# The first block's mixer: half of the conditioning's steps on GpSimd, a new order on VectorE, and the gate's rows ahead of the state's products

## The reference

```python
# first stage, two blocks (l = 0, 1); the second block's feed-forward is a mixture of 8 experts
mod = c @ w_ada[l] + b_ada[l]        # the "conditioning": 6144 columns, six parts of 1024
h = x * (1 + scale) + shift
p = h @ w_in[l]                      # retention q,k,v,gate | state's x,B,C,z,dt | attention q,k,v
mixed = [retention(...), ssd(...), window_attention(...)] @ w_out[l]
x = layernorm(ALPHA * x + (1 + gate) * mixed)
x = layernorm(ALPHA * x + (1 + gate2) * ffn(modulated x))
# second stage: two more blocks (mLSTM, convolution, cross-attention, feed-forward)
```

## Time and profile before

| | |
|---|---|
| median of 3 runs | 2784.83 us |
| the profiled execution | 2773.45 us |
| its span, first to last instruction | 2771.6 us |
| TensorE busy | 2663.4 us (96%) |
| VectorE busy | 2196.3 us (79%) |
| ScalarE busy | 1520.4 us (55%) |
| GpSimd busy | 50.1 us (2%), 83 instructions |
| TensorE's mean granted clock | 0.972 of full speed |

### The profile page before, as it was taken

How to read it: one execution, slowest core, us unless ns; L and a number is a source line. 1 busy time by engine, 2 the same in 40 slices (tenths; PEclk the granted TensorE clock), 3 DMA queues, 4 the chain that set the end, 5 groups by cost and what they waited for, 6 DMA issues and landing times.

```text
span 2771.6 us, 37886 instructions
## 1 busy us (share of the span) xinstructions
PE 2663.4 (96%) x15712; PEld 2363.7 (85%) x15712; DVE 2196.3 (79%) x2513; ACT 1520.4 (55%) x1567; POOL 50.1 (2%) x83
## 2 busy tenths in 40 slices
PE   6889999979999999999999989999999999999998
PEld 5778998768888888888888779999899999998898
DVE  7877777768888898988888878895487789954777
ACT  3424345437767777677777755544455564444554
POOL 2000000000000000000000000000000000000000
PEclk9879999999999999999999999999999999999999
DMA  8739875269999999999999943446355543544453
GB/s 311 250 129 339 321 250 175 96 198 363 349 356 349 349 360 347 360 347 357 349 360 345 365 157 106 134 152 210 127 199 183 174 149 115 168 152 154 166 183 114
DMA packets 376065, 669.86 MB, mean 242 GB/s; under 512 B 26825, under 2 KB 199503, under 8 KB 371023
## 3 DMA queue, kind: packets, MB, share of 16 engines
q1 hardware_dynamic: 358400, 662.55, 68.0%
q10 hardware_dynamic: 17487, 4.83, 0.7%
HBM read 663.13 MB, written 4.19 MB: 241 GB/s over the span
## 4 chain that ended last, share of the span: by engine, by line
PE 85%; DVE 9%; ACT 2%; issue 1%; DMA 1%; POOL 0%; ACTq 0%; DVEq 0%; POOLq 0%
PE PS L444 24%; PE PS L446 24%; PE PS L445 24%; PE PS L544 2%; DVE LO L439 2%; PE PS L1629 2%; PE PS L2464 2%; DVE AR L2753 1%; DMA RAW<-in_w_ada_dram 1%; PE PS L1860 1%; ACT HI L430 1%; PE PS L2350 1%; PE PS L1896 1%; DVE RAW L697 1%; DVE AR L697 1%
## 5 line engine op out<-in xcount | busy, mean ns | idle before, releaser
L439 DVE TENSOR_TENSOR LO<-RAW,HI 128x2048 fp32r<-128x2048 f32 x410 | 930.7, 2275 | 238.0 <-ACT HI L430 237.9
L430 ACT ACTIVATE HI<-RAW 128x2048 fp32r<-128x2048 f32 x410 | 780.2, 1904 | 351.2 <-PE PS L446 307.2
L444 PE MATMUL PS<-X1H,HI 128*128 128x256 f32 (+1 forms) x2128 | 610.7, 287 | 10.6 <-DVE X1L L584 4.8
L445 PE MATMUL PS<-X1L,HI 128*128 128x256 f32 (+1 forms) x2128 | 604.5, 284 | 0.0
L446 PE MATMUL PS<-X1H,LO 128*128 128x256 f32 (+1 forms) x2128 | 604.4, 284 | 0.0
L444 PE MATMUL PS<-HI,X1H 128*128 128x512 f32 x1056 | 431.1, 408 | 3.5 <-DVE LO L439 3.5
L444 PEld LDWEIGHTS PS<-X1H,HI 128*128 128x128 f32 (+1 forms) x2128 | 408.8, 192 | 15.8 <-issue 8.6
L446 PE MATMUL PS<-HI,X1L 128*128 128x512 f32 x1056 | 414.0, 392 | 0.0
L445 PE MATMUL PS<-LO,X1H 128*128 128x512 f32 x1056 | 413.0, 391 | 0.0
L445 PEld LDWEIGHTS PS<-X1L,HI 128*128 128x128 f32 (+1 forms) x2128 | 408.9, 192 | 2.0
L446 PEld LDWEIGHTS PS<-X1H,LO 128*128 128x128 f32 (+1 forms) x2128 | 408.7, 192 | 0.7
(11 more groups left out here) (392 smaller groups left out, 2891.9 us busy)
## 6 DMA issues: line engine op xcount, KB each, us to landing
RAW<-in_w_in_dram SPq DMA_DIRECT2D x66, 1024.0 KB, 5.2
RAW<-in_expert_w_gate_dram SPq DMA_DIRECT2D x66, 1024.0 KB, 5.2
RAW<-in_expert_w_up_dram SPq DMA_DIRECT2D x64, 1024.0 KB, 5.2
RAW<-in_expert_w_down_dram SPq DMA_DIRECT2D x62, 1024.0 KB, 5.4
RAW<-in_ffn_w_up_dram SPq DMA_DIRECT2D x55, 1024.0 KB, 5.6
AR<-in_expert_w_down_dram SPq DMA_DIRECT2D x50, 1024.0 KB, 5.4
AR<-in_expert_w_up_dram SPq DMA_DIRECT2D x48, 1024.0 KB, 5.5
AR<-in_expert_w_gate_dram SPq DMA_DIRECT2D x46, 1024.0 KB, 5.3
```

Of the source, the lines that this page charges most:

```text
L430: a.activation(HI[:, n % NH, 0:size(i)], raw_at(i), ACT.Copy).then_inc(*hi.up(i))
L439: v.tensor_tensor(LO[:, m % NH, 0:n], raw_at(i), HI[:, m % NH, 0:n].bitcast(F32), ALU.subtract).then_inc(*lo.up(i))
L444: t.matmul(o, lh, rh, start=first, stop=False)
L445: t.matmul(o, lh, rl, start=False, stop=False)
```

## The change

1. **Half of the steps on GpSimd.** The odd steps (columns 1024 to 2047) go to GpSimd. `scalar_tensor_tensor` is replaced there by two instructions: a multiply in place in the landing slot, and an addition. VectorE keeps the even steps. GpSimd does k = 0 to 8 from the mixer's start, k = 9 and 10 between the root for `retvar` and that for `ssdvar`, k = 11 to 15 behind that one, ahead of the residual's roots.
2. **VectorE's order.** The splits, the rotation, the softmax's maxima and the decays of `dve_mixer1` stand in another order, for both blocks. Before, `ada()` did a pair; now one step, spread over sixteen places, four of them behind `dve_fm_scaled`; the last one stands behind the split of the feed-forward's first gate tile and ahead of the residual.
3. **TensorE.** The sum over partitions of the first conditioning block moves from behind `logits(3)` to behind `ret_scores(3)`. `pe_rows` stands ahead of the state's 24 products `y` (L1134, L1136) instead of behind them.
4. **ScalarE.** The eviction of retention's q and k and of r1 stands ahead of the softmax's exponentials; the rows' eviction ahead of the squares (L1273).
5. **SyncE.** `SIDE_AFTER` issues the pairs later.

```diff
     def ada_load(s, m):
         if prev is not None:
-            s.wait_ge(*dve_ada("step", prev))
+            s.wait_ge(*ada_stepped(prev))      # pool_ada for an odd step, dve_ada for an even one
...
+    def pool_ada_step(g, m):
+        l, b, k, c0, cols, sl, slot, acc, _, acc_user = ADA[m]
+        g.wait_ge(*ada_in[sl](m))
+        o = acc[:, c0:c0 + cols]
+        if k == 0:
+            if acc_user is not None:
+                g.wait_ge(*pe_ada("sum", acc_user))
+            g.wait_ge(*act_front("param", 0))
+            g.tensor_scalar(o, slot, pcol("c", 0), None, ALU.mult).then_inc(*pool_ada.up("step", m))
+        else:
+            g.tensor_scalar(slot, slot, pcol("c", k), None, ALU.mult).then_inc(*pool_ada.up())
+            g.wait_ge(*pool_ada.last())
+            g.tensor_tensor(o, o, slot, ALU.add).then_inc(*pool_ada.up("step", m))
...
     def pe_ada_sum(t, n, bank):
-        t.wait_ge(*dve_ada("step", ADA_OF[n]))
+        if n in (1, 2):
+            t.wait_ge(*dve_ada("step", ADA_OF[n] - 1))
+        t.wait_ge(*ada_stepped(ADA_OF[n]))
...
     pe_mixer1:
-        if l == 0:                              # behind logits(3)
-            t.wait_ge(*dve_mix("lg", l, 1))
-            pe_ada_sum(t, 1, 3)
...
         ret_scores(3)
+        if l == 0:
+            t.wait_ge(*dve_mix("lg", l, 1))
+            pe_ada_sum(t, 1, 3)
...
         z.then_inc(*pe_mix.up("pv", l))
+        t.wait_ge(*act_ev(f"in{l}r2", 1))
+        pe_rows(t, (l, 0))
         t.wait_ge(*dve_mix("gate", l, 1))
...
-        t.wait_ge(*act_ev(f"in{l}r2", 1))       # behind the products y
-        pe_rows(t, (l, 0))
...
     dve_mixer1: (ada() is now one even step)
         split_lo(v)                             # k
-        ada()
+        split_lo(v)                             # v
         conv(1)
-        split_lo(v)
         ada()
-        conv(2)
-        split_lo(v)
-        ada()
+        split_lo(v)
         v.tensor_copy(CS, PS[:, 3, 0:16]).then_inc(*dve_mix.up("cs", l))
-        split_lo(v)
-        ada()
+        conv(2)
...
         logits(3)
+        if l == 0:
+            dve_cosine(v)
+        rotate()
+        split_lo(v)
         v.tensor_reduce(mx[:, 0:4], LG[:, :, 0:128], AX, ALU.max)
...
         gate(1)
-        ada()
+        v.wait_ge(*pe_mix("pt", l, 3))
+        dve_diag(v, (l, 0), MOD[:, l, 16:24])
...
         v.tensor_scalar(v8, v8, 1.0 / 64, None, ALU.mult).then_inc(*dve_mix.up("retvar", l))
+        ada()
+        split_lo(v)                             # out a
...
-        dve_diag(v, (l, 0), MOD[:, l, 16:24])   # behind "swa"
+        ada()
...                                             # the state's y, gated
-        split_lo(v)
         ada()
+        split_lo(v)                             # out b
...                                             # "ssd", dve_fm_scaled
+        ada()
         split_lo(v)                             # out c
+        ada()
         split_lo(v)                             # out d
+        ada()
+        split_lo(v)                             # the feed-forward's first gate tile
+        ada()
...
     gpsimd_program:
+            if l == 0:
+                for k in range(9):
+                    pool_ada_step(g, 9 + 2 * k)
             g.wait_ge(*dve_mix("retvar", l))
             pool_rsqrt(g, v8, v8, LN_EPS, "ret", l)
+            if l == 0:
+                for k in range(9, 11):
+                    pool_ada_step(g, 9 + 2 * k)
             g.wait_ge(*act_mix("ssdvar", l))
             pool_rsqrt(g, m4, m4, LN_EPS, "ssd", l)
+            if l == 0:
+                for k in range(11, 16):
+                    pool_ada_step(g, 9 + 2 * k)
             pool_residual(g, l, 0)
...
-    SIDE_AFTER = {1: (0,), 4: (1,), 5: (2,), 6: (3,), 7: (4,), 8: (5,), 9: (6,), 10: (7,), 11: (8,), 13: (9, 10),
-                  14: (11, 12), 15: (13, 14), 16: (15,)}
+    SIDE_AFTER = {1: (0,), 4: (1,), 5: (2,), 6: (3,), 8: (4,), 10: (5,), 11: (6,), 12: (7,), 13: (8,), 14: (9, 10),
+                  15: (11, 12), 16: (13, 14, 15)}
```

More of the change, by code:

```diff
@@ L310, in emit_program @@
     pe_front, act_front, dve_front = sig("pe_front"), sig("act_front"), sig("dve_front")
-    pe_ada, dve_ada = sig("pe_ada"), sig("dve_ada")
+    pe_ada, dve_ada, pool_ada = sig("pe_ada"), sig("dve_ada"), sig("pool_ada")
     pe_mix, act_mix, dve_mix, pool_mix = sig("pe_mix"), sig("act_mix"), sig("dve_mix"), sig("pool_mix")
@@ L409, in load @@
         elif slot_of[i] in (2, 3):
-            s.wait_ge(*dve_ada("step", ADA1 - 1))
+            s.wait_ge(*ada_stepped(ADA1 - 1))
             s.wait_ge(*pe_ada("sum", 2))
@@ L675, in emit_program, with ada_stepped @@
     ADA1 = ADA_OF[2] + 1
+    def ada_stepped(m):
+        return pool_ada("step", m) if ADA[m][3] else dve_ada("step", m)
     def ada_load(s, m):
@@ L695, in ada_step @@
         else:
-            v.wait_ge(*dve_ada("step", m - 1))
+            v.wait_ge(*dve_ada("step", m - (2 if cols < 2048 else 1)))
             v.scalar_tensor_tensor(o, slot, pcol("c", k), o, ALU.mult, ALU.add).then_inc(*dve_ada.up("step", m))
+    def pool_ada_step(g, m):
[11 more added lines that the diff above has]
+            g.tensor_tensor(o, o, slot, ALU.add).then_inc(*pool_ada.up("step", m))
     def pe_ada_first(t, bank):
@@ L1036, in turn_probs @@
                 t.wait_ge(*dve_mix("den", l))
+            if h == 1 and l == 0:
+                t.wait_ge(*dve_ada("mod", 1))
             if h > 1:
@@ L1245, in act_mixer1 @@
         split_hi(a)
+        for cp in range(2):
+            a.wait_ge(*pe_mix("qt", l, cp))
+            a.activation(QT1[:, 2 * cp:2 * cp + 2, :], PS[:, 6 + cp, :].rearrange("p (c n) -> p c n", c=2),
+                         ACT.Copy).then_inc(*act_mix.up("qt", l, cp))
+        rows(1, R[:, :, 512:1024], ACT.Copy)
+        split_hi(a)
         a.wait_ge(*dve_mix("sink", l))
@@ L1252, in act_mixer1 @@
         z.then_inc(*act_mix.up("probs", l))
-        split_hi(a)
-        for cp in range(2):
-            a.wait_ge(*pe_mix("qt", l, cp))
-            a.activation(QT1[:, 2 * cp:2 * cp + 2, :], PS[:, 6 + cp, :].rearrange("p (c n) -> p c n", c=2),
-                         ACT.Copy).then_inc(*act_mix.up("qt", l, cp))
-        rows(1, R[:, :, 512:1024], ACT.Copy)
         decay(0)
@@ L1269, in act_mixer1 @@
         split_hi(a)
+        act_residual(a, l, 0)
         for k in range(2):
@@ L1275, in act_mixer1 @@
         z.then_inc(*act_mix.up("ssdvar", l))
-        act_residual(a, l, 0)
         act_fm_scaled(a, ("mix", l), [2, 3, 0, 1], X2H, lambda c: pcol(f"ssd_norm{l}", c - 2) if 2 <= c < 6 else None, MIXED)
@@ L1295, in ada @@
                 ada_step(v, 8 + side[0])
-                ada_step(v, 9 + side[0])
                 side[0] += 2
@@ L1423, in dve_mixer1 @@
         split_lo(v)
-        ada()
-        v.wait_ge(*act_mix("xs", l, 3))
-        v.tensor_tensor(XD.rearrange("p t (h d) -> p t h d", h=8), XS.rearrange("p t (h d) -> p t h d", h=8),
-                        view(DTt, [8, 2], [1, 8], [0, 64]), ALU.mult).then_inc(*dve_mix.up("xd", l))
-        v.wait_ge(*act_mix("probs", l))
-        v.wait_ge(*act_mix("ek", l))
-        v.tensor_tensor(den, den, ek, ALU.add).then_inc(*dve_mix.up())
-        v.wait_ge(*dve_mix.last())
-        v.reciprocal(den, den).then_inc(*dve_mix.up("den", l))
         decay(4)
@@ L1438, in dve_mixer1 @@
         split_lo(v)
-        ada()
+        v.wait_ge(*act_mix("probs", l))
+        v.wait_ge(*act_mix("ek", l))
+        v.tensor_tensor(den, den, ek, ALU.add).then_inc(*dve_mix.up())
+        v.wait_ge(*dve_mix.last())
+        v.reciprocal(den, den).then_inc(*dve_mix.up("den", l))
         decay(6)
@@ L1443, in dve_mixer1 @@
         ret_decay(3)
+        if l == 0:
+            dve_ada_sum(v, 1, 3)
         ada()
-        split_lo(v)
+        v.wait_ge(*act_mix("xs", l, 3))
+        v.tensor_tensor(XD.rearrange("p t (h d) -> p t h d", h=8), XS.rearrange("p t (h d) -> p t h d", h=8),
+                        view(DTt, [8, 2], [1, 8], [0, 64]), ALU.mult).then_inc(*dve_mix.up("xd", l))
         h8 = lambda a: a.rearrange("p t (h d) -> p t h d", h=8)
```

8 lines of the change are left out of this document (1 added, 7 removed).

## The result

The changed kernel takes 2809.89 us (median of 4 runs, 2803.13 to 2814.79), the kernel before on the same chip 2784.21 us: ratio 1.0091 (95% interval 1.0069 to 1.0113), 25.7 us more. The forecast was 2783.1 us with a range up to 2796.

A forecast was written before the change was run, and what follows sets the result against it. TensorE, busy 96%, was taken as the bound, with the first normalisation's shift deciding: variance -23.8, tail +25.6, second block -3.5, in all -1.7 us, giving a median of 2783.1 us; range 2773 to 2796.

The forecast's parts named there:

- What bounds the kernel: Whole span: TensorE busy for 96%; the first block's gain or loss is the shift of its normalisation start at 208.0 us.
- The price of GpSimd's multiply: GpSimd's conditioning step, 1024 elements: multiply 1.1 us, 2.6 at the other end; whole step 3.4 us, or 5.0.
- The variance at 140: End of retention's variance in the first block: 140 us, between 134 and 145.0, 23.8 us earlier than 163.8.
- the template: Second block's same stretch, 89.6 us, adjusted to 91.4 for the first block: variance at 132.0 us at the earliest.
- rival 1: VectorE held for the full length of GpSimd's instructions, up to the variance and in the tail: +8.5 us, 2793; chance 0.25.
- The tail: First block, variance to normalisation: GpSimd's chain of loads and steps makes it 69.8 us, before 44.2, so 25.6 longer.
- What else is moved costs nothing: First block's tail: moved rows and earlier `y` lie in the time in which TensorE waits for the tail; no cost.
- It decides from a cycle of about 8.3 us on: Rival 1's threshold: GpSimd's load-and-step cycle behind the variance, forecast 7.25 us, from which the kernel counts as slower.
- The second block: Second block's mixer, order change only: two stalls of 3.6 us removed, counted as 3.5 us gained, bounds 0 and 4.5.
- the list of signs: Trace signs: TensorE idle under 8 us, gate load 42 to 48 us behind the variance; wrong if step over 5 us.

The follow-up runs named there:

- e9: Changed kernel with GpSimd's steps, from the second of a block on, on 640 of 1024 columns, the other 384 left out of the sums; 2787.8 us, ratio 1.0028.
- e2: Changed kernel with every conditioning step on VectorE, the changed order and queue kept; 2781.2 us, 0.9991 of the kernel before.
- e6: Changed kernel with VectorE doing both steps of a pair up to k = 8, GpSimd its half only from k = 9; 2799.3 us, ratio 1.0056.
- e14: e8 with both pair 9's step and the split behind the variance moved ahead of the gates of the state's products; 2770.5 us, ratio 0.9949.
- e3: Kernel before, all steps on VectorE, plus GpSimd work on its own tile behind pairs 0 to 13 that nobody waits for; 2808.9 us, ratio 1.0090.
- e4: Kernel before, in its old order and queue, with only the odd steps given to GpSimd; 2806.3 us, ratio 1.0088.
- e7: Changed kernel with GpSimd doing 640 of the 1024 columns of its steps and VectorE the other 384; 2804.7 us, ratio 1.0070.
- e5: Changed kernel with GpSimd doing its half only up to k = 8, VectorE both steps of a pair from k = 9; 2795.5 us, ratio 1.0046.
- e1: Changed kernel with loads of pairs 14 and 15 issued behind the feed-forward's first two tiles instead of ahead; 2808.2 us, ratio 1.0091.
- e10: e2 plus GpSimd multiplies and subtractions on its own tile at the odd loads of pairs 1 to 7, which nobody waits for; 2787.8 us, ratio 1.0023.
- e8: e2 with the feed-forward's first gate tile split behind the residual instead of ahead of the last pair's step; 2772.7 us, ratio 0.9956.

## Why the prediction was wrong

**What bounds the kernel: right.** The first block's mixer and the shift of the first normalisation carried the result, +25.4 us at the normalisation, of the median's +25.7.

**The price of GpSimd's multiply: the step that failed.** "I take 1.1 and keep 2.6 for the range." It is 2.85 us for 1024 elements, above even the other end; the addition was right (2.3 forecast, 2.34 measured). The row of the small dependent multiplies, with its slope of 2.3 ns an element, was the better guide (its 2.6 us is 0.25 short), and the memset the wrong one: it writes and reads nothing. The step is 5.3 us, not 3.4. The normalisation was missed by 23.6 us (233.4 against 140 + 69.8 = 209.8). e9, which has a step of 3.4, is at 215.9, so this term is worth 17.5 of them, 6.8 ahead of the variance and 10.7 in the tail; 6.1 are left, 2.7 and 3.4, within what two traces differ by.

**The variance at 140: measured 149.5.** The 140 was 132 by the template and 8 for holding, between nothing and the full 13. For the step as it was drawn this came out near, 142.7 in e9. That is in part luck, since the 132 is not borne out: e2 and e6, where GpSimd does nothing up to the variance, end it at 140.9 and 140.0, with the odd steps on VectorE, and by the prediction's own count VectorE had 14 us free for their 9.7. No run has neither the odd steps nor GpSimd's work. I left open whether VectorE waits for GpSimd; it does, for up to the whole instruction. Two groups of VectorE by form, from 40.6 to 124 us, in e2 and then in the changed kernel (busy, mean ns):

```profile
L439 DVE TENSOR_TENSOR LO<-AR,HI 128x2048 fp32r<-128x2048 f32 x2 | 4.6, 2288 | 2.8 <-ACT HI L430 2.8
...
L1375 DVE TENSOR_TENSOR AR<-AR,SM 128x512 f32<-128x512 f32 x4 | 2.5, 688 | 0.1
```

```profile
L439 DVE TENSOR_TENSOR LO<-AR,HI 128x2048 fp32r<-128x2048 f32 x2 | 6.7, 3363 | 2.8 <-ACT HI L430 2.8
...
L1374 DVE TENSOR_TENSOR AR<-AR,SM 128x512 f32<-128x512 f32 x4 | 4.7, 1236 | 0.1
```

Up to the first sum VectorE is busy for 69.6 us in e2 (114 instructions) and 73.5 in the changed kernel (106 instructions, window 40.6 to 130.5). The eight odd steps that it gave away had cost 9.7 (seven of 1.28 us and the multiply of 0.7), so what was left became 73.5 - (69.6 - 9.7) = 13.6 us longer. The engine that was to be relieved ended up with more busy time, by 3.9 us, and TensorE's products ahead of the sum end 4.6 us later than in e2. In e9, with the shorter step, VectorE is busy for 66.6 us, so what was left became 6.7 longer.

The step that failed has a second effect, which the prediction did not have at all: the sum over partitions waits for GpSimd's step k = 7, 2.1 us, and TensorE's clock is low behind that wait, 1.9 us more (the rows of the first sum above).

That a VectorE instruction with two SBUF inputs and a GpSimd one that reads SBUF block each other, the later one fully, is the rule of the Trainium skill ("SBUF — State Buffer", Who interferes with whom) that the prediction quoted. The trace agrees in both directions (2.28 to 4.45 us on VectorE, 2.85 to 5.59 on GpSimd).

This was rival 1, with its place and its sign; its price, +8.5 us, was too low since it had the cheap multiply or the blocking, not both at full size. It was also added up too low: 64.5 us, a full split of 2.2 in each of six steps, and 2.3 more are 80.0, not "about 76", and the rival went on with 75. With 80 it is 145 + 80 = 225, +13.5 us after the second block's 3.5, some 2798, already beyond the range's end of 2796.

**The tail: right chain, wrong size.** The size is for the most part that of the step, seven times (10.7 of the 14.1 us, by e9). Queue, single slots and the residual behind the gate tile's split are as drawn. Forecast 69.8, measured 83.9, term by term: root and what is around it 2.2, measured 4.9; from k = 9 to the load of pair 15, 39.7, measured 53.7 (154.46 to 208.1); gate tile from there to its split's end 11.1, measured 14.6; the rest 11.5, measured 10.7; the 5.3 allowed for holding is inside the measured terms. One thing was not in it: the gate's rows stand on ScalarE behind the split of tile c, which SyncE issued only at 160.1; TensorE waited 15.2 us there. "What else is moved costs nothing" holds in the changed kernel only because the chain of steps ends later still; in e14, where this wait is gone, the tail is the shortest of the new order.

**"It decides from a cycle of about 8.3 us on".** The cycle is 9.5, and the kernel is slower. Where the limit lies was not measured; e9, with 7.7, is already slower than before (1.0015 to 1.0042).

**The second block: right in kind, over half in size.** 87.5 us against 89.6: 2.1, forecast 3.5. The other kernels agree: from the second block's first memset on GpSimd to retention's root it takes 89.4 to 89.8 us in the three kernels with the old order (before, e3, e4) and 87.1 to 87.6 with the new one (88.5 in e7). The root's first instruction now meets a split there, 2.21 instead of 0.25 us.

**Of the list of signs**, the multiply, the step of over 5 us, the splits that lengthen, and the load of the gate tile (60 us behind the variance, not 42 to 48) all said "wrong". TensorE's idle time up to the variance fell from 15.9 to 11.0 us (108.9 - 97.9), not to under 8. The residual did start behind its split, and the second block's stalls are gone.

The variance of the changed kernel and of e5 differ by 3.0 us with the same program up to there. Of these, 1.4 us lie ahead of the sum over partitions, which starts at 125.8 and 127.2, and 1.6 in the sum and behind it (5.28 instead of 4.55 us, and 20.0 instead of 19.1 to the variance), where TensorE's clock stays low for longer: from 130 to 140 us it was granted 0.74 of full speed in the changed kernel, 0.53 in e5 and 0.50 in e1. The wait ahead of the sum was 3.0 us in e5 and e1 against 2.1. What made the first 1.4 us, and whether the longer wait is what kept the clock low for longer, stays open. Putting GpSimd's multiply on ScalarE wasn't tried.

## What to carry to other kernels

Work given to GpSimd beside a nearly full VectorE is not fully parallel where both read SBUF tiles: here VectorE's other instructions became longer by a sixth to a third of GpSimd's busy time (8.6 us for 53.6 in e10, 6.7 for 34.6 in e9, 13.6 for 46.2 in the changed kernel). In a chain of single-slot loads and steps, price the slower engine's step times the number of links before anything else, and count how many links a new order leaves behind the point that it brings forward. A tile's load has two locks, its place in the queue and the release of its slot; moving one did little here while the other held (issue at 147.3 us in e8, 144.5 and 142.95 with one moved, 133.4 with both).

## What the runs showed of the hardware

- GpSimd's multiply of a tile by a column of scalars: 1.25 us for 384 elements a partition, 1.88 for 640, 2.85 for 1024, so about 2.5 ns for each further element; the addition of two tiles 1.53 for 640 and 2.34 for 1024, 2.1 ns. The one with a single tile as input is the slower one. VectorE does both at once, for 1024, in 1.28 us.
- Holding goes both ways and up to the length of the other's instruction: a split of VectorE of 2.28 us took 4.45, an instruction of 16 elements 2.21 instead of 0.18. It can be more than one instruction: GpSimd's multiply took 5.59 instead of 2.85 us beside the end of a step and a whole split of VectorE (117.07 to 120.54).
- 53.6 us of GpSimd's busy time (held time included) on data of its own cost VectorE 8.6 us of longer instructions (e10).
- A wait of 2.1 us of TensorE was followed by a stretch at the lower clock, in which a matmul of 512 columns took 0.63 us instead of 0.39 (changed kernel, up to 135 us); in e2 and e10, where the same sum starts without a wait, it takes 3.73 us instead of 4.55.
